# Attention stage: the older row's product moved between the turns, and ScalarE's read of it moved ahead

## The reference

```python
def _diff_attend(q, k, v, q_pos, k_pos, lam):
    s = jnp.einsum('bqhmd,bkhmd->bhmqk', q, k).astype(jnp.float32) * (DH_B ** -0.5)
    mask = k_pos[None, :] <= q_pos[:, None]
    p = jax.nn.softmax(jnp.where(mask, s, -jnp.inf), axis=-1)
    a = p[:, :, 0] - lam * p[:, :, 1]
    return jnp.einsum('bhqk,bkhe->bqhe', a.astype(v.dtype), v)
```

## Time and profile before

| | us |
|---|---|
| median of 3 runs | 3445.84 |
| lowest and highest | 3441.09, 3450.5 |
| the profiled execution | 3448.67 |
| its span | 3446.9 |
| TensorE busy in the span | 3036.4 (88%) |
| VectorE busy | 1543.0 (45%) |
| ScalarE busy | 1079.5 (31%) |
| mean granted clock of TensorE | 0.94 |

### The profile page before, as it was taken

One profiled execution on the slowest core, in us unless ns is written; L12 is line 12 of the kernel. 1 busy time (PEld: TensorE's weight loads), 2 busy tenths in 40 slices (PEclk: granted clock), 3 DMA queues, 4 the chain that ended last, 5 costly groups with the idle time before them and its releaser, 6 DMA issues. The chain is left out here.

```text
span 3446.9 us, 51390 instructions
## 1 busy us (share of the span) xinstructions
PE 3036.4 (88%) x19556; PEld 2758.2 (80%) x19556; DVE 1543.0 (45%) x2276; ACT 1079.5 (31%) x1984; POOL 131.5 (4%) x139
## 2 busy tenths in 40 slices
PE   4699976888799999999998989587699999999997
PEld 2699963444599999999996989366388999999996
DVE  2244123554465444444456110486547444444446
ACT  4211211334543233323334211343335332333322
POOL 1000000000000000000000000253000000000000
PEclk7799997888899999999999999799799999999998
DMA  4243154874231111111112211233323111111113
GB/s 168 102 155 120 55 196 153 293 268 150 89 119 41 49 43 43 42 43 49 43 53 107 106 43 62 101 110 118 132 86 115 49 37 43 49 43 49 37 43 112
DMA packets 145263, 319.82 MB, mean 93 GB/s; under 512 B 12434, under 2 KB 78451, under 8 KB 136707
## 3 DMA queue, kind: packets, MB, share of 16 engines
q1 hardware_dynamic: 104450, 249.29, 21.1%
q10 hardware_dynamic: 40704, 69.09, 5.7%
HBM read 272.69 MB, written 45.64 MB: 92 GB/s over the span
## 5 line engine op out<-in xcount | busy, mean ns | idle before, releaser
L510 PE MATMUL f_acc<-h_hi,f_hi 128*128 128x352 f32 x1632 | 539.2, 330 | 13.9 <-issue 6.6
L510 PE MATMUL f_acc<-h_hi,f_lo 128*128 128x352 f32 x1632 | 532.7, 326 | 0.0
L510 PE MATMUL f_acc<-h_lo,f_hi 128*128 128x352 f32 x1632 | 529.9, 325 | 0.0
L510 PE MATMUL f_acc<-m_hi,f_hi 128*128 128x352 f32 x1248 | 410.1, 329 | 4.3 <-DVE m_lo L1588 3.3
L510 PE MATMUL f_acc<-m_hi,f_lo 128*128 128x352 f32 x1248 | 405.1, 325 | 0.0
L510 PE MATMUL f_acc<-m_lo,f_hi 128*128 128x352 f32 x1248 | 402.7, 323 | 0.0
L510 PE MATMUL f_acc<-f_ghi,f_hi 128*128 128x352 f32 x1056 | 345.4, 327 | 39.1 <-DVE y L1675 32.9
L510 PE MATMUL f_acc<-f_glo,f_hi 128*128 128x352 f32 x1056 | 340.7, 323 | 0.0
L510 PE MATMUL f_acc<-f_ghi,f_lo 128*128 128x352 f32 x1056 | 340.1, 322 | 0.0
L1675 DVE TENSOR_TENSOR y<-y,f_acc 128x1056 f32<-128x1056 f32 x160 | 198.6, 1252 | 298.9 <-PE f_acc L510 298.9
L510 PEld LDWEIGHTS f_acc<-h_hi,f_hi 128*128 128x128 f32 x1632 | 311.9, 191 | 17.1 <-issue 9.4
(11 more groups left out here) (360 smaller groups left out, 5109.9 us busy)
## 6 DMA issues: line engine op xcount, KB each, us to landing
f_st<-w_ffn SPq DMA_DIRECT2D x132, 512.0 KB, 3.4
kt<-cache_k SPq DMA_DIRECT2D x128, 256.0 KB, 5.2
att_vt<-cache_v SPq DMA_DIRECT2D x128, 256.0 KB, 5.5
gla_ada_w<-w_ada SPq DMA_DIRECT2D x16, 1024.0 KB, 5.6
x<-y ACTq DMA_DIRECT2D x9, 1408.0 KB, 6.0
ret_ada_w<-w_ada ACTq DMA_DIRECT2D x12, 1024.0 KB, 6.0
y<-w_qkv SPq DMA_DIRECT2D x10, 1024.0 KB, 6.2
ada_ada_w<-w_ada SPq DMA_DIRECT2D x8, 1024.0 KB, 4.8
```

The lines of the kernel that those rows point to most:

```text
L510: last = nc.tensor.matmul(out, a(kk), b(kk), start=(n == 0), stop=(n == 3 * nk - 1))
```

## The change

TensorE's step is now: scores (s), the first group of turns (s-2), the product (s-3), the second group of turns (s-2) if there is one, the cached part (s). ScalarE's step is now: the cached scale, the read of the product (s-4), the reads of turns (s-2), the exponentials (s), the cached exponentials or take. A table `ROW_BLOCKS` is put in for the number of the row block, with the values 0 to 7 in order, so that `row_block(s)` is `s % 8` as before. No duration, size or wait is changed. The added lines move the line numbers after L2045 down by 1 to 6.

```diff
@@ -2045,6 +2045,7 @@
+    ROW_BLOCKS = list(range(NCH))
...
+        def row_block(s):
+            return ROW_BLOCKS[s % NCH]
...
         def batches(s):
-            return s % NCH // BT + 1
+            return row_block(s) // BT + 1
...
@@ -2223,12 +2228,13 @@
                     if s < STEPS:
                         score(i, s)
                     if 2 <= s < STEPS + 2:
-                        for c in range(batches(s - 2)):
-                            turn(i, s - 2, c)
+                        turn(i, s - 2, 0)
+                    if s >= 3:
+                        product(i, s - 3)
+                    if 2 <= s < STEPS + 2 and batches(s - 2) > 1:
+                        turn(i, s - 2, 1)
                     if s < STEPS:
                         (cached_scores, cached_turns, cached_products, cached_picks)[s % WIN](i, s // WIN)
-                    if s >= 3:
-                        product(i, s - 3)
...
@@ -2412,11 +2418,11 @@
                     if s < STEPS and s % WIN == 3:
                         cached_scale(i, s // WIN)
+                    if s >= 4:
+                        take_product(i, s - 4)
                     if 2 <= s < STEPS + 2:
                         for c in range(batches(s - 2)):
                             take_turned(i, s - 2, c)
-                    if s >= 4:
-                        take_product(i, s - 4)
```

More of the change, by code:

```diff
@@ L2134, in score @@
             def score(i, s):
-                u, qb = divmod(s, NCH)
+                u, qb = s // NCH, row_block(s)
                 L = (qb + 1) * CH
@@ L2154, in turn @@
                 pe.wait_ge(aready, i * PASS_BT + (batch_at(s) + c + 1))
-                for j in range(c * BT, min(c * BT + BT, s % NCH + 1)):
+                for j in range(c * BT, min(c * BT + BT, row_block(s) + 1)):
                     last = nc.tensor.transpose(ps_t[:, j % BT, :], p[s % 3][:, j * CH:(j + 1) * CH], g.ident())
@@ L2159, in product @@
             def product(i, s):
-                u, qb = divmod(s, NCH)
-                if qb == 0:
+                u, qb = s // NCH, row_block(s)
+                if s % NCH == 0:
                     pe.wait_ge(v_in[u], i * 16 + 16)
@@ L2244, in masked_max @@
             def masked_max(i, s):
-                qb = s % NCH
+                qb = row_block(s)
                 L = (qb + 1) * CH
@@ L2260, in mix @@
             def mix(i, s):
-                L = (s % NCH + 1) * CH
+                L = (row_block(s) + 1) * CH
                 link = i * (LINKS * STEPS) + (LINKS * s + 4)
@@ L2379, in take_turned @@
                     act.wait_ge(summed, i * STEPS + (s + 1 + STEPS - 2))
-                n = min(BT, s % NCH + 1 - c * BT)
+                n = min(BT, row_block(s) + 1 - c * BT)
                 nc.scalar.activation(aT[s % 2][:, c * BT:c * BT + n, :], ps_t[:, 0:n, :], ACT.Copy).then_inc(aready, 1)
             def take_product(i, s):
-                u, qb = divmod(s, NCH)
+                u, qb = s // NCH, row_block(s)
                 act.wait_ge(summed, i * STEPS + (s + 1 + STEPS))
```

## The result

| | before | changed |
|---|---|---|
| median of 5 runs, us | 3445.84 | 3428.48 |
| lowest and highest | 3438.14, 3454.5 | 3422.76, 3429.05 |
| span of the profiled execution | 3446.9 | 3426.6 |
| attention stage, first scores to the end of the last product | 283.3 | 267.0 |

In the profiled executions the stage gives 16.3 of 20.3 us. Another 3.5 lie ahead of it, where nothing was changed (the stage starts at 564.6 instead of 568.1), and starts between 563.0 and 568.4 are seen in the other profiles of both kernels, so that part is scatter.

The account below looks back on a forecast made before the run. TensorE was taken as the fullest engine, 81% busy in the stage, with 13.3 us of waits for ScalarE within reach. Chain 4.55 (2.6 and 1.95 by pass) plus clock 1.0 gave 3440 us, range 3430 to 3451.

Parts of the forecast that it names:

- the clock's term: Granted clock in the attention stage: 1.0 us better taken, between ends of 10.5 better and 8 worse.
- the bound (10.5 better): Four places of cached products kept at full rate, 7 us, with the second pass's end 3 to 4 more.
- Rival 1: The clock holds throughout the stage: full bound of 4.55 + 10.5 = 15 us, 3431; chance 0.16.
- Steps 7 and 8: Product (4) between the turns makes ScalarE's exponentials 0.45 late; cached scores of step 8 later: loss 0.85 us a pass.
- Steps 9 to 11: Cached products start 1.45 us later, but product (7), 2.0 us, is gone from behind them: gain 0.5 a pass.
- Step 12: Product (9) now stands ahead of the cached scores, where TensorE leads: loss 0.65 us a pass.
- Steps 6 and 14: Product fills both TensorE waits before the cached products, so the next scores come earlier: gain 1.1 us each.
- End of a pass: Chain from step 15's exponentials to product (15) falls from 10.8 to 9.4 us: gain 1.4 a pass.
- The signs that the prediction named: Wrong if step 9's exponentials are not later, step 12's cached scores end no later, or stage clock leaves 0.82 to 0.88.
- Rival 2: The wait only moves: cached weights come later and the product waits for ScalarE; 0 won, 3446; chance 0.22.
- Rival 3: Slower: longer waits in steps 9 and 10 let the clock fall, 4 us each pass; 7.5 worse, 3453; chance 0.10.
- its trigger: TensorE's waits in steps 9 and 10, one of 0.2 and two of 1.4 us, being enough for the clock to fall.

Follow-up runs that it names:

- steps 6 to 14 filled: Kernel before plus unread 384-column matmuls between turn groups in steps 6, 14 and before cached weights in 6, 10, 14: 3432.89 us against 3442.32, ratio 0.9968.
- the tiny matmuls: Kernel before plus unread matmuls 4 columns wide, in the waits of steps 6, 10 and 14: 3446.89 us against 3444.62, ratio 1.0007.
- the version with the end filled: Kernel before plus unread matmuls of 384 or 256 columns in the waits behind step 15 of each pass: 3437.84 us against 3446.42, ratio 0.9980.

## Why the prediction was wrong

The direction and most of the map of the steps were right. The forecast failed at the clock's term, taken as 1.0 us, and at two terms of the chain, the loss of steps 7 and 8 and the gain at a pass's end.

- **The clock, taken as 1.0, was 8.2 in the stage.** The prediction had the bound (10.5 better) and the places (four of cached products, the second pass's end) and then took a value near the small end, as if the places were chance. Mostly they are not: in two profiles the kernel before had 3 and 4 of the 4 places slow and the second pass's end slow both times, the changed kernel none in two. Five places go from slow to full: 1.67, 1.70 and 1.36 us in the cached products, 4.7 at the end, and the cached scores of step 8 in the second pass, 5.25 to 3.64, that I had not listed. The first pass gives 1.3 there, too, but product (5) just ahead ran at 2.71 for 1.50. Some 3.5 us are given back: 1.1 in step 2 of the second pass (5.21 to 6.35), 0.9 in step 1 of that pass, whose scores take 1.37 for 0.70, and 1.4 in product (7) of the first (2.05 to 3.47). With the cached scores and the scores ahead of them, step 12 gains 2.1 in the first pass and loses 1.2 in the second. Rival 1, with 0.16, comes nearest, and its 3431 is near by luck in part: of its 10.5 of clock 8.2 came, and its chain of 4.55 was 3.5 too small.
- **Steps 7 and 8: loss of 0.85 forecast, none measured.** The cached scores of step 8 begin 9.56 us after step 7's scores in the second pass (757.57 to 767.13), before 9.54. The step that failed is the 0.45 for ScalarE's exponentials (its own terms, 0.58 less 0.16, give 0.42): in the first pass they start 4.41 us after the scores, before 4.39. I took product (4) at its busy time of 1.35, but in the row behind the turns it takes 1.19 start to start (632.79 to 633.98), and ScalarE saves the two hand-overs with the read of the product, 0.29. Product (5) took 1.34 start to start, not 1.60 (765.24 to 766.58). In the first pass the cached scores of step 8 do come 1.5 later (630.26 to 641.31), but there the turns and product (5) ran at the lower clock.
- **Steps 9 to 11: 0.5 forecast, 0.8 measured.** 2.0 less 1.17 (10.89 - 9.72), without what product (7) lost to the clock in the first pass. The new waits are near the forecast, and so are the exponentials of step 9: they start 5.6 us after the end of the cached scores, before 4.9, so 0.7 later where I had 0.87.
- **Step 12: -0.65 forecast, about -0.85 measured** (scores of step 11 to cached scores 6.88 before and 7.39 after, while the scores between took 0.34 less through the clock).
- **Steps 6 and 14: 1.1 forecast, 1.09 measured** (end of step 4's cached scores to step 7's scores, 17.08 and 15.99).
- **End of a pass: 1.4 forecast, 2.2 measured** (17.31 to 15.12). All of it is ScalarE's edit, which alone gives 2.11. From the end of step 15's exponentials to the end of product (15) it is 8.5 us where I summed 9.0: rows of matmuls that follow each other overlap, and I added busy times. The exponentials are not late either, where I had 0.3: they end 6.7 us after their scores in both kernels.

The chain comes to 1.1 + 0 + 0.8 - 0.85 + 1.1 + 2.2 = 4.35 in the first pass and 3.5 in the second, 7.9, beside 8.1 by the measure. Forecast were 4.55. That the two agree so well is luck: by pass the measure gives 5.5 and 2.5. Either way chain and clock have about half each of the stage's 16.3.

The signs that the prediction named for its being wrong hardly caught this. The exponentials of step 9 are late. In step 12 the cached scores end later against the scores of step 11 in the second pass (13.55 us for 11.51); only in the first, through the clock, do they end earlier (11.94 for 13.21). And the stage's clock, 0.87, lies within the 0.82 to 0.88 that were allowed, though the step from 0.84 to 0.87 is 8 us. What did show it was the stage's length, 267 where 279 to 283 was expected, and 16.2 us of waits on the product's read where some 8 were: steps 5, 6, 13 and 14 have one of 0.7 each that was not counted.

Rival 2 (the wait only moves) is right on these two waits, 11.5 us more in one for 12.0 less in the other, and wrong on the time. Rival 3 met its trigger, waits of 1.55 and 1.10 in steps 9 and 10, and in the first pass product (7) did run at 3.47 instead of 2.02; the cached products behind it stayed at 3.64, and no loss of 4 us a pass came. In the version with the product only between the groups they did fall, to 6.18 and 6.44, behind a wait of 2.54.

One thing stays open: when the clock falls at the end of a pass in the old order. The waits there are the same each time, and in the four profiles with TensorE's and ScalarE's old order and nothing added at the end the eight ends fare differently. Two are at full rate throughout (first pass of before, second with steps 6 to 14 filled). Two lose one product (product (13) at 2.56 in the first pass with steps 6 to 14 filled, product (14) at 3.14 in the second with the tiny matmuls). The other four are slow in the last two products at the least. With ScalarE's edit and nothing added at the end it is 2 of 16, with one product of 2.9 us each, and in the two kernels with matmuls added there none of 4. So fewer and fuller waits at the end make a fall rarer. Why one end falls and the next like it does not is not shown; that it hangs on when the work before it falls in time would explain it, and no run tests that. How much of the median the ends are worth is known only from the version with the end filled, 0.20%.

## What to carry to other kernels

A short wait of TensorE costs twice where it makes the clock fall: look in the stretch view for the places where like matmuls take 5.3 and 3.6 us, take a second profile, and price the places that are slow in both at their full cost. Work moved into the waits ahead of a long matmul group can be worth more than the wait itself (here 1.1 us of chain and up to 1.7 of clock in each place), and matmuls whose result is thrown away are a quick test of how much. When an instruction moves ahead on one engine, move its reader ahead too; here the reader's move alone gave 0.34% of the 0.53%.

## What the runs showed of the hardware

Waits under 1 us, two or three close together, can be followed by a fall of the granted clock from 2.4 to 1.2 GHz. In step 14 of the kernel before it fell behind waits of 0.95 and 0.89 us, and at the end of the second pass behind 0.94 and 0.84. They don't always do it: in step 6 of the first pass the same two waits left the clock at 1.00 in one profile and not in the other. Two matmuls of 0.81 us in these waits held it in all four places of one profile, and two of 0.28 us in none. Turns run at both rates. Four blocks take 0.66 us at full clock, and at 0.50, in the slow end of the second pass of the kernel before,

```profile
839.88 1.06 PE L2156 MATMUL att_ps_t<-const,att_p 128*128 128x128 f32 x4
```
